# One ring of ten buffers for the u and v rows of the experts, in the order in which GpSimd asks for them

## The chip, the cores and the metric

The kernel runs on one core of one Trainium2 chip. A core has five engines that run their own instruction streams and meet at semaphores: TensorE (PE; its weight loads are listed apart as PEld), VectorE (DVE), ScalarE (ACT), GpSimd (POOL) and SyncE (SP). Sixteen DMA engines move data between HBM and the on-chip memory. The metric is the device time of one execution in microseconds (us); lower is better.

## The reference, cut to what matters

Two layers of a trunk over 256 context and 256 latent tokens of width 1024. Each layer has a block of token mixers and then a layer of experts; in the second layer only the latent tokens go through the experts. The experts are the part that the change touches:

```python
def peer(h, wq, subkeys, u_tab, v_tab):
    ...
    best, pos = lax.top_k(cand, PEER_TOPK)              # 16 experts for each token and each of 8 heads
    idx = jnp.take_along_axis(cidx, pos, axis=-1)       # numbers among 128 * 128 = 16384 experts
    g = jax.nn.softmax(best, axis=-1)
    ...
        act = jax.nn.gelu(jnp.einsum('thkd,td->thk', u_tab[ib], hb))
        return jnp.einsum('thk,thkd->td', (gb * act).astype(v_tab.dtype), v_tab[ib])
```

For every token, head and chosen expert one row of 1024 float32 of the table u is fetched and dotted with the token's activation, and one row of the table v is fetched and added with the weight `g * gelu(dot)`. The tables stay in HBM, 64 MB each for one layer; only the chosen rows are read.

## The kernel before, in words

`build` runs, one after the other: `begin`, `opening` (mixers of layer 0), `experts_beside` (experts of layer 0 for 512 tokens, with the rest of the layer's mixers and the first part of layer 1 woven in), `closing` (the rest of the mixers of layer 1), `experts` (experts of layer 1 for the 256 latent tokens) and `store`. Each of these is a block that ends in a barrier of all engines. In a block each engine has its instructions in a fixed order, written out tick by tick by the parts' methods.

The class `Peer` is the expert layer. 128 tokens lie on the 128 partitions. One tick has two halves: the even half handles the u row number n, the odd half the v row number n - LV, with LV = 20. A row here means one gather: 128 table rows, one to a partition, 128 x 1024 float32, 0.524 MB. In `experts_beside` there are 512 u rows and 512 v rows, in `experts` 256 of each. A window of 16 rows belongs to one head.

- GpSimd issues the gathers, in one stream: `ask_u` (line 1862) and `ask_v` (line 1875). For the first 20 ticks it asks for u rows alone (u0 to u19), then for one u and one v in turn (u20, v0, u21, v1, ...), and for the last 20 for v rows alone.
- VectorE dots each u row with the tokens' activation (`dot`, line 2109, counted by `u_dotted`), and between dots it goes through the choice of the experts of later windows (`choose`, which ends in line 2217 and counts `chosen_done`; the first u row of a window waits for that).
- TensorE adds v rows in pairs (`add_v`, line 2002, counted by `v_summed`, one count for two rows). For the first pair of each window it needs the window's weights, which are transposed by line 1981 and copied by ScalarE (line 2075).
- After the last pair of 128 tokens ScalarE copies the sums (line 2064), TensorE transposes them (lines 1964, 1967) and VectorE adds them to the residual (line 2118). After the last pair of a block this is followed by the barrier and the next block.

Before the change u rows have five buffers and v rows have five others (`RU, RV`). The u row n is asked for once the u row n - 5 has been dotted; the v row v once the pair that holds the row v - 5 has been summed. The projection beside the experts loads its weights on SP's queue (`arena<-in_w_in`, line 565) and multiplies in line 595.

Of the kernel before, what the change touches and what calls it, by code (L numbers as in the profile page):

```python
# [19 lines left out]
P = 128  # L20
D = 1024
# [1706 lines left out]
class Peer(Part):  # L1728
# [3 lines left out]

    RU, RV, LV = 5, 5, 20

    def __init__(self, nc, sems, m, mod, d, l, passes, h, x, banks, after, kept=1):
        self.nc, self.m, self.mod, self.d, self.l, self.passes, self.h, self.x = nc, m, mod, d, l, passes, h, x
        self.after, self.kept = after, kept
        self.QB, self.TB = banks  # L1740
        self.W = 16 * len(passes)
        self.n = 16 * self.W
        self.ticks = 2 * (HEAD + self.n + 34)
        self.kind = [1 if lo < CTX else 0 for lo in passes]
        self.u_rows = d["peer_u"].rearrange("l e n -> (l e) n")
        self.v_rows = d["peer_v"].rearrange("l e n -> (l e) n")
        (self.sk_turned, self.sk_out, self.q_mult, self.q_out, self.s_mult, self.s_out, self.s_used,
         self.diffed, self.g_exp, self.shared, self.chosen_done, self.u_dotted, self.gelu_done,
         self.key_masked, self.rows_known, self.coef_masked, self.spread, self.weights_out,
         self.v_summed, self.h_turned, self.h_out, self.o_copied, self.o_turned, self.o_added, *rest) = sems(  # L1750
             "sk_turned", "sk_out", "q_mult", "q_out", "s_mult", "s_out", "s_used", "diffed", "g_exp",
             "shared", "chosen_done", "u_dotted", "gelu_done", "key_masked", "rows_known",
             "coef_masked", "spread", "weights_out", "v_summed", "h_turned", "h_out",
             "o_copied", "o_turned", "o_added", *[f"wq_in{r}" for r in range(2 * kept)],
             *[f"sk_in{r}" for r in range(2)], *[f"u_in{r}" for r in range(self.RU)], *[f"v_in{r}" for r in range(self.RV)])
        K = 2 * kept
        self.wq_in, self.sk_in, rest = rest[:K], rest[K:K + 2], rest[K + 2:]
        self.u_in, self.v_in = rest[:self.RU], rest[self.RU:]
        self.own = sems.own
        self.turned_keys = self.turned_queries = self.turned_rows = self.turned_out = 0  # L1760
        self.spread_keys = self.spread_coefs = 0
        self.normed = []
        self.choosing = None
# [82 lines left out]
    def gpsimd(self, pool, i):  # L1846
# [4 lines left out]
        else:  # L1851
            self.ask_v(pool, i // 2 - HEAD)

    def ask_u(self, pool, n):
        nc, x = self.nc, self.x
        if 0 <= n < self.n:
            w, q = divmod(n, 16)
            if q == 0:
                pool.wait_ge(self.chosen_done, w + 1)
            if n >= self.RU:  # L1860
                pool.wait_ge(self.u_dotted, n - self.RU + 1)
            nc.gpsimd.indirect_dma_start(x.us[:, n % self.RU, :], None, self.u_rows, bass.IndirectOffsetOnAxis(  # L1862
                x.chosen[:, w, q:q + 1], 0)).then_inc(self.u_in[n % self.RU], 16)

    def ask_v(self, pool, n):
        nc, x = self.nc, self.x
        v = n - self.LV
        if 0 <= v < self.n:
            w = v // 16
            c, r = self.place(v)  # L1870
            if v % 16 == 0:
                pool.wait_ge(self.rows_known, w + 1)
            if v >= self.RV:
                pool.wait_ge(self.v_summed, (v - self.RV) // 2 + 1)
            nc.gpsimd.indirect_dma_start(x.vs[:, v % self.RV, :], None, self.v_rows, bass.IndirectOffsetOnAxis(  # L1875
                x.rows[:, w % 4, 4 * c + r:4 * c + r + 1], 0)).then_inc(self.v_in[v % self.RV], 16)

    def free_turns(self, pe):

# [105 lines left out]
    def add_v(self, pe, n):  # L1985
# [7 lines left out]
        if v % 16 == 1:  # L1993
            pe.wait_ge(self.weights_out, g + 1)
        for a in (v - 1, v):
            pe.wait_ge(self.v_in[a % self.RV], 16 * (a // self.RV + 1))
        flat = x.wts[:, g % 2, :, :].rearrange("p r n -> p (r n)")
        for half in range(2):
            for a in (v - 1, v):
                c, r = self.place(a)  # L2000
                to = 32 * ((c + 2 * half) % 4)
                ins = nc.tensor.matmul(m.ps[to:to + 32, half, :], flat[:, r * P + 32 * c:r * P + 32 * c + 32],  # L2002
                                       x.vs[:, a % self.RV, half * BANK:(half + 1) * BANK], start=a % 128 < 4,
                                       stop=a % 128 >= 124)
        ins.then_inc(self.v_summed, 1)

# [92 lines left out]
    def dot(self, dve, n):  # L2099
        nc, m, x = self.nc, self.m, self.x  # L2100
        if 0 <= n < self.n:
# [2 lines left out]
            g = n // 16  # L2104
            if n % 16 == 0 and g >= 4:
                dve.wait_ge(self.gelu_done, g - 3)
            dve.wait_ge(self.u_in[n % self.RU], 16 * (n // self.RU + 1))
            u, at = x.us[:, n % self.RU, :], 16 * (g % 4) + n % 16
            nc.vector.tensor_tensor_reduce(u, u, x.ht, 1.0, 0.0, ALU.mult, ALU.add, x.dots[:, at:at + 1]  # L2109
                                           ).then_inc(self.u_dotted, 1)  # L2110
        for half, at in ((0, 156), (1, 158)):
# [111 lines left out]

def peer_memory(sb, passes, kept=1):
    x = Mem()
    x.us, x.vs = sb("u_rows", [P, Peer.RU, D]), sb("v_rows", [P, Peer.RV, D])
    x.ht, x.ob = sb("h_rows", [P, D]), sb("out_rows", [P, D])
    x.wq, x.sk, x.skT = sb("wq", [P, kept, 2, KD // 2, T]), sb("subkeys", [P, 2, 2, P]), sb("subkeysT", [P, 2, P])
    x.q0, x.q1 = sb("q0", [P, 2, P]), sb("q1", [P, PH, 2, P])
# [430 lines left out]
```

## Time and profile before

| | us |
|---|---|
| median of 3 runs | 3344.3 (3339.93 to 3347.95) |
| profiled execution | 3360.33, of which 3358.2 lie between its first and its last instruction |
| GpSimd's first u row, `experts_beside` | at 610.75 |
| end of the last v pair there | at 2338.95 |
| GpSimd's first u row, `experts` | at 2624.50 |
| end of the last v pair there | at 3339.38 |

Busy shares of the span: TensorE 69%, VectorE 55%, GpSimd 52%, ScalarE 18%. The 16 DMA engines moved 1028.53 MB at 306 GB/s over the span, 847.35 MB of it on the queue that GpSimd fills. The shares are averages over stages that have different limits, so the stages are read one by one: by the busy time of each engine and the DMA share in chosen stretches of time, by who waited for whom, and by the instructions of an engine in order of time.

### The profile page before, as it was taken

Reading aid. Unit: us, or ns where it says so; the run is one execution under the profiler, and the core shown is the slowest. Engines: PE = TensorE matmul, PEld = TensorE weight load, DVE = VectorE, ACT = ScalarE, POOL = GpSimd, SP = SyncE. Lnnn points to the kernel's source line nnn. Section 1 sums busy time; section 2 is a strip of 40 time slices with the busy share of each in tenths; the row PEclk is TensorE's granted clock in tenths of the full one; section 3 lists DMA queues with packets and bytes.
Section 4 is the critical chain, followed back from the end, with each engine's and each line's share of the span. In section 5 each row is a group of like instructions: output and inputs, shape, how many; then the busy total and the mean of one; then the engine's idle time right before and its main releaser. Section 6 shows DMA issues by size and latency. Waiting matters only on the chain. (4 is left out here: it accounts for less than half of the span.)

```text
span 3358.2 us, 31993 instructions
## 1 busy us (share of the span) xinstructions
PE 2308.6 (69%) x10877; PEld 1384.0 (41%) x10877; DVE 1848.4 (55%) x4792; ACT 617.1 (18%) x1252; POOL 1733.9 (52%) x1580
## 2 busy tenths in 40 slices
PE   5999999878856887565776577554798555444434
PEld 3676677634524654223553255321567322101001
DVE  1324334677775566775546754672434766666651
ACT  2113432124111121111102121110241111110000
POOL 0001000467775566776667666774000577777774
PEclk7999989978668998677887688765788766555555
DMA  7576222899999999999999899997303999999997
GB/s 282 178 267 237 86 63 97 303 365 373 334 374 352 354 383 361 378 370 362 352 343 369 307 396 388 393 379 267 112 1 108 309 395 403 406 389 393 389 380 255
DMA packets 395064, 1028.53 MB, mean 306 GB/s; under 512 B 31890, under 2 KB 176282, under 8 KB 393754
## 3 DMA queue, kind: packets, MB, share of 16 engines
q0 software_dynamic: 232064, 847.35, 66.4%
q1 hardware_dynamic: 162794, 179.15, 16.0%
q8 instruction: 89, 1.46, 0.2%
q14 instruction: 69, 0.57, 0.0%
q10 hardware_dynamic: 48, 0.01, 0.0%
HBM read 1019.05 MB, written 7.34 MB: 306 GB/s over the span
## 5 line engine op out<-in xcount | busy, mean ns | idle before, releaser
L1862 POOL DMA_INDIRECT u_rows<-in_peer_u,chosen x768 | 860.9, 1121 | 866.1 <-DVE chosen L2217 585.3
L2109 DVE CUSTOM_DVE_ANT_0 u_rows<-u_rows,h_rows 128x1024 f32<-128x1024 f32 x768 | 935.8, 1222 | 559.3 <-DMA u_rows<-in_peer_u,chosen 539.6
L1875 POOL DMA_INDIRECT v_rows<-in_peer_v,row_of x768 | 844.0, 1099 | 445.7 <-PE ps L2002 248.9
L2002 PE MATMUL ps<-v_rows,weights 128*32 128x512 f32 x3072 | 588.6, 848 | 697.2 <-DMA v_rows<-in_peer_v,row_of 694.6
L2002 PEld LDWEIGHTS ps<-v_rows,weights 128*32 128x32 f32 x3072 | 76.7, 124 | 978.7 <-issue 959.8
L1556 PE MATMUL ps<-front,arena 128*128 128x256 f32 x1536 | 389.6, 411 | 75.5 <-DMA arena<-in_w_in 74.6
L1556 PEld LDWEIGHTS ps<-front,arena 128*128 128x128 f32 x1536 | 311.9, 207 | 160.4 <-DMA arena<-in_w_in 62.0
L595 PE MATMUL ps<-front,arena 128*128 128x256 f32 (+1 forms) x816 | 202.4, 407 | 45.3 <-DMA arena<-in_w_in 41.4
L1930 PE MATMUL ps<-h,wq 128*128 128x256 f32 x768 | 199.2, 413 | 5.4 <-ACT h L439 3.7
L595 PEld LDWEIGHTS ps<-front,arena 128*128 128x128 f32 (+1 forms) x816 | 160.2, 200 | 91.4 <-issue 35.0
L1930 PEld LDWEIGHTS ps<-h,wq 128*128 128x128 f32 x768 | 155.0, 209 | 55.4 <-issue 31.3
L361 POOL DMA_DIRECT2D arena<-in_ada_w x40 | 28.9, 722 | 287.8 <-PE ps L384 247.0
L1571 ACT COPY arena<-ps 128x256 f32<-128x256 f32 x96 | 35.9, 374 | 327.4 <-PE ps L1556 327.3
L2075 ACT COPY weights<-ps 128x128 f32<-128x128 f32 x48 | 12.8, 267 | 342.7 <-DVE row_of L2152 270.2
L2053 ACT ACTIVATE gelu<-dots 128x16 f32<-128x16 f32 x48 | 10.4, 216 | 344.0 <-DVE dots L2109 343.9
L2118 DVE SCALAR_TENSOR_TENSOR resid<-ps,mod,resid 128x128 f32<-128x128 f32 x48 | 13.5, 344 | 108.4 <-PE ps L1964 86.3
L2035 ACT COPY scores<-ps 128x256 f32<-128x256 f32 x48 | 17.9, 372 | 292.8 <-PE ps L1944 292.8
L629 DVE COPY front<-ps 128x256 f32<-128x256 f32 (+2 forms) x28 | 11.8, 422 | 108.6 <-PE ps L595 98.9
L831 DVE RECIPROCAL arena<-arena 96x512 f32<-96x512 f32 (+2 forms) x21 | 63.9, 3041 | 10.6 <-ACT arena L741 10.1
L943 DVE TENSOR_REDUCE arena<-ps 128x1 f32<-128x512 f32 (+1 forms) x48 | 28.8, 600 | 73.6 <-PE ps L893 73.0
L2020 ACT COPY subkeysT<-ps 128x256 f32<-128x256 f32 x48 | 17.8, 371 | 271.8 <-PE ps L1909 271.8
L1642 PE MATMUL ps<-front,arena 128*128 128x256 f32 x256 | 63.7, 400 | 4.4 <-DVE arena L1658 1.5
(356 smaller groups left out, 3213.4 us busy)
## 6 DMA issues: line engine op xcount, KB each, us to landing
arena<-in_w_in SPq DMA_DIRECT2D x79, 1024.0 KB, 13.6
arena<-in_ada_w POOLq DMA_DIRECT2D x40, 1024.0 KB, 6.6
wq<-in_peer_wq SPq DMA_DIRECT2D x48, 512.0 KB, 9.2
arena<-in_w_out SPq DMA_DIRECT2D x12, 1024.0 KB, 7.3
u_rows<-in_peer_u,chosen POOLq DMA_INDIRECT x768, 6.8
v_rows<-in_peer_v,row_of POOLq DMA_INDIRECT x768, 6.6
ada_w<-in_ada_w SPq DMA_DIRECT2D x4, 2048.0 KB, 23.2
arena<-in_w_branch SPq DMA_DIRECT2D x16, 512.0 KB, 3.6
```

What stands on the lines that cost most here:

```text
L361: pool.dma_start(self.raw[:, j % self.RING, :, :], weights.rearrange("(k p) n -> p k n", p=P)[:, k0:k0 + 2, lo:lo + MROUND]).then_inc(self ...
L595: ins = nc.tensor.matmul(m.ps[0:n, bank, 0:T], w, h[:, k, :], start=(k == 0), stop=(k == KD - 1))
L831: self.own.link(nc.vector.reciprocal(self.tile(x.rs2, j), self.tile(x.rs2, j)))
L943: self.own.link(nc.vector.reduce_max(x.st[:, 2, u:u + 1], m.ps[:, self.S, 0:n], axis=AX.X))
L1556: ins = nc.tensor.matmul(m.ps[:, self.banks[i % 2], 0:T], self.ring[:, (c + self.flip) % 2, k, (i % 2) * P:(i % 2 + 1) * P], self.f.h[:, k ...
L1571: nc.scalar.copy(self.sig[:, j % self.room, :], self.m.ps[:, self.banks[j % 2], 0:T]).then_inc(self.out, 1)
L1642: ins = nc.tensor.matmul(m.ps[:, self.banks[n % 2], 0:T], self.wb[:, n // 4 % 2, a, (k % 4) * P:(k % 4 + 1) * P], self.f.yT[:, i, a, :], s ...
L1862: nc.gpsimd.indirect_dma_start(x.us[:, n % self.RU, :], None, self.u_rows, bass.IndirectOffsetOnAxis(x.chosen[:, w, q:q + 1], 0)).then_inc ...
L1875: nc.gpsimd.indirect_dma_start(x.vs[:, v % self.RV, :], None, self.v_rows, bass.IndirectOffsetOnAxis(x.rows[:, w % 4, 4 * c + r:4 * c + r ...
L1930: ins = nc.tensor.matmul(m.ps[:, self.QB + c, 0:T], x.wq[:, b, part, k, c * P:(c + 1) * P], self.h[:, 4 * part + k, :], start=(part == 0 a ...
L2002: ins = nc.tensor.matmul(m.ps[to:to + 32, half, :], flat[:, r * P + 32 * c:r * P + 32 * c + 32], x.vs[:, a % self.RV, half * BANK:(half + ...
L2109: nc.vector.tensor_tensor_reduce(u, u, x.ht, 1.0, 0.0, ALU.mult, ALU.add, x.dots[:, at:at + 1]).then_inc(self.u_dotted, 1)
```

## The change

The two sets of five buffers become one of ten. The list `asked` holds all rows in the order in which GpSimd asks for them: u alone, then u and v in turn, then v alone. The row at place j of the list uses the buffer j mod 10, and it is asked for once the row at place j - 10 has been used: dotted, if that was a u row, or summed with its pair, if it was a v row. In the middle of the list the place j - 10 is the row of the same kind five before, which is what the row waited for already. In the first 20 places the ring holds u rows alone, so u10 waits for u0 instead of u5; u20 (place 20) waits for u10, v0 (place 21) for u11, and so on up to v4 (place 29) for u19. In the last 20 places v rows alone are asked for, and they wait in turn for the last u rows and for v rows up to ten before.

```diff
-    RU, RV, LV = 5, 5, 20
+    R, LV = 10, 20
...
-        self.u_in, self.v_in = rest[:self.RU], rest[self.RU:]
+        self.row_in = rest
+        self.asked = []
+        for n in range(self.n + self.LV):
+            self.asked += [("u", n)] if n < self.n else []
+            self.asked += [("v", n - self.LV)] if n >= self.LV else []
+        self.place_of = {row: j for j, row in enumerate(self.asked)}
...
+    def take(self, pool, j):
+
+        if j >= self.R:
+            kind, a = self.asked[j - self.R]
+            if kind == "u":
+                pool.wait_ge(self.u_dotted, a + 1)
+            else:
+                pool.wait_ge(self.v_summed, a // 2 + 1)
+
+    def landed(self, j):
+
+        return self.row_in[j % self.R], 16 * (j // self.R + 1)
...
-            if n >= self.RU:
-                pool.wait_ge(self.u_dotted, n - self.RU + 1)
-            nc.gpsimd.indirect_dma_start(x.us[:, n % self.RU, :], None, self.u_rows, bass.IndirectOffsetOnAxis(
-                x.chosen[:, w, q:q + 1], 0)).then_inc(self.u_in[n % self.RU], 16)
+            j = self.place_of["u", n]
+            self.take(pool, j)
+            nc.gpsimd.indirect_dma_start(x.ring[:, j % self.R, :], None, self.u_rows, bass.IndirectOffsetOnAxis(
+                x.chosen[:, w, q:q + 1], 0)).then_inc(self.row_in[j % self.R], 16)
...
-            if v >= self.RV:
-                pool.wait_ge(self.v_summed, (v - self.RV) // 2 + 1)
-            nc.gpsimd.indirect_dma_start(x.vs[:, v % self.RV, :], None, self.v_rows, bass.IndirectOffsetOnAxis(
-                x.rows[:, w % 4, 4 * c + r:4 * c + r + 1], 0)).then_inc(self.v_in[v % self.RV], 16)
+            j = self.place_of["v", v]
+            self.take(pool, j)
+            nc.gpsimd.indirect_dma_start(x.ring[:, j % self.R, :], None, self.v_rows, bass.IndirectOffsetOnAxis(
+                x.rows[:, w % 4, 4 * c + r:4 * c + r + 1], 0)).then_inc(self.row_in[j % self.R], 16)
...
-            pe.wait_ge(self.v_in[a % self.RV], 16 * (a // self.RV + 1))
+            pe.wait_ge(*self.landed(self.place_of["v", a]))
...
-            dve.wait_ge(self.u_in[n % self.RU], 16 * (n // self.RU + 1))
-            u, at = x.us[:, n % self.RU, :], 16 * (g % 4) + n % 16
+            j = self.place_of["u", n]
+            dve.wait_ge(*self.landed(j))
+            u, at = x.ring[:, j % self.R, :], 16 * (g % 4) + n % 16
...
-    x.us, x.vs = sb("u_rows", [P, Peer.RU, D]), sb("v_rows", [P, Peer.RV, D])
+    x.ring = sb("expert_rows", [P, Peer.R, D])
```

No engine has more or fewer instructions, and none changes its order; the semaphores are as many as before. What changes is the semaphore and the count for which GpSimd's gathers wait at the two ends of the list, and the place of a row in memory.

GpSimd at the start of an expert block. The names of the semaphores are those that the same numbers had earlier in the program: m_placed_1 is `chosen_done`, m_in0_1 is `u_dotted`, m_in3_1 is `rows_known`, stored_9 is `v_summed`. A row ending in x11 stands for eleven instructions. Before:

```order
L1862 DMA u_rows<-in_peer_u,chosen 128x1024 [waits m_placed_1]
L1862 DMA u_rows<-in_peer_u,chosen 128x1024 x4
L1862 DMA u_rows<-in_peer_u,chosen 128x1024 [waits m_in0_1] x11
L1862 DMA u_rows<-in_peer_u,chosen 128x1024 [waits m_in0_1,m_placed_1]
L1862 DMA u_rows<-in_peer_u,chosen 128x1024 [waits m_in0_1] x4
L1875 DMA v_rows<-in_peer_v,row_of 128x1024 [waits m_in3_1]
L1862 DMA u_rows<-in_peer_u,chosen 128x1024 [waits m_in0_1]
L1875 DMA v_rows<-in_peer_v,row_of 128x1024
```

and now, at the same place:

```order
L1880 DMA expert_rows<-in_peer_u,chosen 128x1024 [waits m_placed_1]
L1880 DMA expert_rows<-in_peer_u,chosen 128x1024 x9
L1880 DMA expert_rows<-in_peer_u,chosen 128x1024 [waits m_in0_1] x6
L1880 DMA expert_rows<-in_peer_u,chosen 128x1024 [waits m_in0_1,m_placed_1]
L1880 DMA expert_rows<-in_peer_u,chosen 128x1024 [waits m_in0_1] x4
L1893 DMA expert_rows<-in_peer_v,row_of 128x1024 [waits m_in0_1,m_in3_1]
L1880 DMA expert_rows<-in_peer_u,chosen 128x1024 [waits m_in0_1]
L1893 DMA expert_rows<-in_peer_v,row_of 128x1024 [waits m_in0_1]
```

Ten u rows instead of five are asked for before the first dot is waited for, and the first v rows now wait for dots.

GpSimd at the end of an expert block, from the last u row on (u511 in `experts_beside`). Before:

```order
L1862 DMA u_rows<-in_peer_u,chosen 128x1024 [waits m_in0_1]
L1875 DMA v_rows<-in_peer_v,row_of 128x1024 [waits stored_9] x5
L1875 DMA v_rows<-in_peer_v,row_of 128x1024 [waits stored_9,m_in3_1]
L1875 DMA v_rows<-in_peer_v,row_of 128x1024 [waits stored_9] x15
L312 UNCONDITIONAL_BRANCH
```

and now:

```order
L1880 DMA expert_rows<-in_peer_u,chosen 128x1024 [waits m_in0_1]
L1893 DMA expert_rows<-in_peer_v,row_of 128x1024 [waits stored_9]
L1893 DMA expert_rows<-in_peer_v,row_of 128x1024 [waits m_in0_1]
L1893 DMA expert_rows<-in_peer_v,row_of 128x1024 [waits stored_9]
L1893 DMA expert_rows<-in_peer_v,row_of 128x1024 [waits m_in0_1]
L1893 DMA expert_rows<-in_peer_v,row_of 128x1024 [waits stored_9]
L1893 DMA expert_rows<-in_peer_v,row_of 128x1024 [waits m_in0_1,m_in3_1]
L1893 DMA expert_rows<-in_peer_v,row_of 128x1024 [waits stored_9]
L1893 DMA expert_rows<-in_peer_v,row_of 128x1024 [waits m_in0_1]
L1893 DMA expert_rows<-in_peer_v,row_of 128x1024 [waits stored_9]
L1893 DMA expert_rows<-in_peer_v,row_of 128x1024 [waits m_in0_1]
L1893 DMA expert_rows<-in_peer_v,row_of 128x1024 [waits stored_9] x11
```

Five of the last twenty v rows now wait for a dot instead of a sum, and the others for a sum that lies up to ten rows back.

## Rows read from the trace of the kernel before

**Rows 1.** Busy us of engines in three stretches; granted clock, DMA share, GB/s.
```profile
1100.00:1350.00 250.00, 208.16 (x989) 142.03 (x987) 156.08 (x421) 48.92 (x85) 162.27 (x141) 0.90 0.99 369
2349.00:2624.00 275.00, 237.28 (x1083) 180.07 (x1084) 113.44 (x303) 83.90 (x184) 0.00 (x0) 0.83 0.28 94
2680.00:3290.00 610.00, 281.65 (x1200) 84.76 (x1198) 394.25 (x1041) 58.77 (x107) 471.61 (x455) 0.56 1.01 394
```

**Rows 2.** The same view of the two ends, where only v rows are asked for.
```profile
2300.00:2337.00 37.00, 18.82 (x81) 2.22 (x74) 0.29 (x2) 0.27 (x1) 15.94 (x17) 0.55 0.79 271
3300.00:3337.40 37.40, 19.76 (x81) 2.49 (x81) 1.70 (x4) 0.48 (x2) 16.59 (x18) 0.50 0.83 279
```

**Rows 3.** GpSimd's waits, 2295 to 2350: total us, times, longest.
```profile
POOL v_rows L1875 <- PE ps L2002: 15.4, 9, 3.0
```

**Rows 4.** GpSimd at the first end: start, us, engine, line, instruction [idle before].
```profile
2298.11 0.94 POOL L1875 DMA_INDIRECT v_rows<-in_peer_v,row_of  x1 [0.31 <-issue]
2302.03 0.94 POOL L1875 DMA_INDIRECT v_rows<-in_peer_v,row_of  x1 [2.97 <-PE ps L2002]
2303.27 0.94 POOL L1875 DMA_INDIRECT v_rows<-in_peer_v,row_of  x1 [0.30 <-issue]
...
2331.83 0.94 POOL L1875 DMA_INDIRECT v_rows<-in_peer_v,row_of  x1 [1.87 <-PE ps L2002]
```

**Rows 5.** The other engines at the first end, same columns.
```profile
2337.02 1.93 PE L2002 MATMUL ps<-v_rows,weights 128*32 128x512 f32 x8 [1.69 <-DMA v_rows<-in_peer_v,row_of]
2339.01 1.07 ACT L2064 COPY out_rows<-ps 128x512 f32<-128x512 f32 x2 [33.44 <-PE ps L2002]
...
2349.35 1.02 SPq L565 DMA_DIRECT2D arena<-in_w_in  x2
```

**Rows 6.** The second end: GpSimd, TensorE and ScalarE, same columns.
```profile
3303.86 0.94 POOL L1875 DMA_INDIRECT v_rows<-in_peer_v,row_of  x1 [3.22 <-PE ps L2002]
...
3332.84 0.94 POOL L1875 DMA_INDIRECT v_rows<-in_peer_v,row_of  x1 [2.39 <-PE ps L2002]
3337.45 1.93 PE L2002 MATMUL ps<-v_rows,weights 128*32 128x512 f32 x8 [1.95 <-DMA v_rows<-in_peer_v,row_of]
3339.44 1.07 ACT L2064 COPY out_rows<-ps 128x512 f32<-128x512 f32 x2 [32.63 <-PE ps L2002]
```

**Rows 7.** DMA issues: KB each, median us from issue to landing.
```profile
v_rows<-in_peer_v,row_of POOLq DMA_INDIRECT x768, 6.6
```

**Rows 8.** GpSimd's waits, 2624 to 2662: total us, times, longest.
```profile
POOL u_rows L1862 <- DVE dots L2109: 3.8, 2, 2.3
```

**Rows 9.** GpSimd and VectorE at the second start, columns as in rows 4.
```profile
2641.96 0.94 POOL L1862 DMA_INDIRECT u_rows<-in_peer_u,chosen  x1 [0.30 <-issue]
2642.89 1.22 DVE L2109 CUSTOM_DVE_ANT_0 u_rows<-u_rows,h_rows 128x1024 f32<-128x1024 f32 x1 [1.37 <-DMA u_rows<-in_peer_u,chosen]
...
2644.39 0.94 POOL L1862 DMA_INDIRECT u_rows<-in_peer_u,chosen  x1 [1.49 <-DVE dots L2109]
...
2645.81 0.17 DVE L2217 TENSOR_SCALAR chosen<-key 128x16 uint32<-128x16 f32 x1
...
2647.24 1.22 DVE L2109 CUSTOM_DVE_ANT_0 u_rows<-u_rows,h_rows 128x1024 f32<-128x1024 f32 x1
...
2647.59 1.68 POOL L1862 DMA_INDIRECT u_rows<-in_peer_u,chosen  x1 [2.26 <-DVE dots L2109]
```

**Rows 10.** GpSimd's waits from 2662 to 3295, the two largest besides "issue".
```profile
POOL v_rows L1875 <- PE ps L2002: 4.3, 14, 0.3
POOL u_rows L1862 <- PE ps L2002: 3.0, 10, 0.3
```

**Rows 11.** GpSimd's waits, 610 to 656, at the first start.
```profile
POOL u_rows L1862 <- DVE dots L2109: 19.1, 11, 5.3
```

**Rows 12.** Two stretches at the first start, columns as in rows 1.
```profile
612.00:678.00 66.00, 54.46 (x240) 45.84 (x241) 48.57 (x140) 6.04 (x16) 36.21 (x34) 0.89 1.02 371
678.00:690.00 12.00, 12.00 (x56) 9.35 (x56) 2.61 (x4) 2.87 (x6) 3.76 (x4) 0.92 0.56 190
```

**Rows 13.** TensorE and GpSimd there, columns as in rows 4.
```profile
674.20 6.56 PE L595 MATMUL ps<-front,arena 128*128 128x256 f32 x16 [5.17 <-DMA arena<-in_w_in]
684.01 0.94 POOL L1875 DMA_INDIRECT v_rows<-in_peer_v,row_of  x1 [9.81 <-PE ps L2002]
```

More of the change, by code:

```diff
@@ L1754, in __init__ @@
              "o_copied", "o_turned", "o_added", *[f"wq_in{r}" for r in range(2 * kept)],
-             *[f"sk_in{r}" for r in range(2)], *[f"u_in{r}" for r in range(self.RU)], *[f"v_in{r}" for r in range(self.RV)])
+             *[f"sk_in{r}" for r in range(2)], *[f"row_in{r}" for r in range(self.R)])
         K = 2 * kept
         self.wq_in, self.sk_in, rest = rest[:K], rest[K:K + 2], rest[K + 2:]
-        self.u_in, self.v_in = rest[:self.RU], rest[self.RU:]
+        self.row_in = rest
[4 more added lines that the diff above has]
+        self.place_of = {row: j for j, row in enumerate(self.asked)}
         self.own = sems.own
@@ L2002, in add_v @@
                 ins = nc.tensor.matmul(m.ps[to:to + 32, half, :], flat[:, r * P + 32 * c:r * P + 32 * c + 32],
-                                       x.vs[:, a % self.RV, half * BANK:(half + 1) * BANK], start=a % 128 < 4,
+                                       x.ring[:, self.place_of["v", a] % self.R, half * BANK:(half + 1) * BANK], start=a % 128 < 4,
                                        stop=a % 128 >= 124)
```

## The prediction, made before the changed kernel was run

> **What bounds the kernel now.** I read the busy time by stretch first, because the shares of the whole span mix stages. In the middle of both expert blocks the 16 DMA engines are full: DMA share 0.99 at 369 GB/s in the first, 1.01 at 394 GB/s in the second, while TensorE, VectorE and GpSimd all have idle time [rows 1]. There only fewer bytes or a better use of the DMA engines could help, and the change moves the same bytes. `closing`, between them, has a DMA share of 0.28 and no GpSimd at all [rows 1], so the change doesn't reach it except by shifting it.
>
> The same view of the two ends, where only v rows are left, shows something else: share 0.79 at 271 GB/s and 0.83 at 279 GB/s [rows 2]. What GpSimd waits for there is TensorE's sum: 15.4 us in 9 waits at the first end [rows 3], seen one by one in its instructions [rows 4]. TensorE in turn waits for v rows to land [rows 5]. That is a circle of ask, landing, sum, ask, which five buffers don't fill. Both ends lie on the path. At the first, the last pair is summed at 2337.02, ScalarE copies the sums at 2339.01, and the next block's first load goes out at 2349.35 [rows 5]. At the second, ScalarE copies right after the last pair [rows 6] and the kernel ends at 3358.2.
>
> **The change, part by part.** *Middle of the lists: nothing.* With u and v in turn, the row ten places back is the row of the same kind five back, so each gather waits for the same count of the same semaphore as before.
>
> *First end, 11.2 us.* v495 is the first row that is held long: it is asked for at 2302.03 after 2.97 us of idle time [rows 4]. An ask that waits for nothing has 0.30 us ahead of it, so in a ring of ten it goes out 2.67 us sooner, at 2299.36. Sixteen rows follow, and unhindered asks start 1.24 us apart (2302.03, 2303.27) [rows 4]: 16 x 1.24 = 19.8, the last ask at 2319.2 instead of 2331.83. With the median of 6.6 us to landing [rows 7] the last row is there at 2325.8. The last sum began at 2337.02 [rows 5], so 11.2 us are gained. The bytes say the same: 37 us at 271 GB/s are 10.03 MB [rows 2]; at the 394 GB/s of the second block [rows 1] they take 25.5 us, to 2325.5. Does the ring of ten hold anything up? v511 waits for the pair of v501, asked for at 2299.36 + 6 x 1.24 = 2306.8, landed at 2313.4 and summed (1.93 us [rows 5]) at 2315.3, 3.9 us before it is needed. TensorE takes 1.93 us for a pair and the DMA engines 2 x 0.524 MB / 394 GB/s = 2.7 us, so TensorE stays behind the data.
>
> *Second end, 10.1 us.* By the same steps: 3303.86 less 3.22 - 0.30 [rows 6] is 3300.94; plus 19.8 and 6.6 makes 3327.4, against a last sum that began at 3337.45 [rows 6]. By bytes: 37.4 us at 279 GB/s are 10.43 MB [rows 2], 26.5 us at 394, which would give 10.9. I take the smaller figure.
>
> Bounds of the two ends. The upper one is by bytes, 11.5 + 10.9 = 22.4. For the lower one, suppose that more rows in flight fill the idle time of the DMA engines but leave their speed while busy: 271 / 0.79 = 343 and 279 / 0.83 = 336 GB/s [rows 2]. Then 10.03 MB take 29.2 us (7.8 gained) and 10.43 MB take 31.0 (6.4 gained), 14.2 in sum. I take 21.3, since the rate of 394 GB/s was held for 610 us by gathers of the same size on the same queue [rows 1].
>
> The row shows 394 GB/s. The Trainium skill, page "DMA: Bandwidth & Descriptors", section "Bandwidth", puts what HBM gives one core at about 358 GB/s. By that figure the ends would take 28.0 and 29.1 us and gain 9.0 + 8.3 = 17.3 instead of 21.3. The trace of the second block does not agree with it, so I leave it out of the sum.
>
> *Second start, 2.4 us.* With ten buffers for u rows alone, two waits for dots go, 3.8 us in all [rows 8], less 2 x 0.30: 3.2 us. Part of it comes back, for an ask that starts while a dot runs takes longer: 1.68 us at 2647.59, inside the dot that began at 2647.24, against 0.94 at 2644.39, outside [rows 9]. Without its wait, u12 starts at 2641.96 + 1.24 = 2643.20, inside the dot of 2642.89 [rows 9], and pays 0.74. That leaves 2.4; with three asks caught it is 1.0, with none 3.2. Next late would be u16, which waits for the choice of the second window: done at 2645.98 [rows 9], while u13 starts at about 2645.2 and u16 three asks later, so it isn't. The gain stays to the end of the block, because from here to 3295 GpSimd never waits more than 0.3 us for a buffer [rows 10] and the DMA engines are full: rows that come earlier leave fewer bytes.
>
> The row shows an ask being held by a dot. The Trainium skill, page "SBUF — State Buffer", section "SBUF: two separate sides", calls the port that VectorE and GpSimd share an exclusive lock, which blocks the loser until the other's instruction ends. By that rule alone u12 would be held from 2643.20 to the dot's end at 2644.11, 0.91 us, and the term would be 2.3.
>
> *First start, 0 us.* GpSimd waits 19.1 us in 11 waits for dots here [rows 11], and they mostly go. But the DMA engines are full all the same, share 1.02 from 612 to 678 [rows 12], with the projection's weights. Rows asked for sooner only push these back. And a stop for all follows: TensorE waits 5.17 us for weights, up to 674.20, and GpSimd waits 9.81 us for TensorE, up to 684.01 [rows 13]. At that point the ring lets GpSimd be no further than before. Bounds: a gain of 3.9 us if the 66 us ran at 394 instead of 371 GB/s; a loss of 6.6 us if all rows that landed after the weights (GpSimd's last ask ended at 674.2, so up to 680.8 by [rows 7]) came before them. I take zero, because a full DMA share says that the order of the bytes changes and not their sum.
>
> *Everything else* is the same instructions in the same order. The new waits of v0 to v4 for dots cost nothing: v4 waits for u19, and u24, asked for just ahead of it, waited for u19 before.
>
> Sum: 11.2 + 10.1 + 2.4 + 0 = 23.7 us off the profiled execution's 3360.3, which makes 3336.6. That execution lies 16 us above the median of the runs; both ends and the start are short stretches that don't scale with it, so I take the same 23.7 off the median: 3344.3 - 23.7 = **3320.6 us**.
>
> **The rivals.** *The ends stay slow.* More rows in flight don't speed up the busy DMA engines: the lower bound, 14.2 + 2.4 = 16.6, gives 3327.7. For it: the low rate while busy at the ends [rows 2]. Against it: that rate comes with few rows in flight, and 394 with more.
>
> *The ends run at the first block's rate.* At 369 GB/s [rows 1] they take 27.2 and 28.3 us, gain 9.8 + 9.1, and with the start 21.3 in all: 3323.0. Against it: the first block shares the engines with the projection's loads, which the ends don't.
>
> *The change doesn't do what it says at the ends.* If the chain there is set by landing alone, so that ten rows in flight each land that much later, only the second start's 2.4 us remain: 3341.9. For it: TensorE's own waits are all for landings. Against it: the DMA share of 0.79 has room.
>
> *Slower by TensorE's clock in `closing`.* This stage starts some 11 us sooner and its matmuls may fall otherwise on the granted clock, whose mean is now 0.83, between the levels of 1.2 and 2.4 GHz. Its 237.28 us of matmul [rows 1] are 237.28 x 0.83 = 197 us at full clock. At a mean of 0.755 they take 261 us, and the 23.7 are gone: that is the point from which it decides. At 0.72 they take 274, a loss of 36 and a net of 12 or 13: 3356.9. Against it: TensorE goes into the block from the same state, 0.50 in both ends' sums [rows 2], and in the same order.
>
> **How the numbers follow.** Forecast 0.60, slow ends 0.20, first block's rate 0.08, no effect at the ends 0.07, clock 0.05. A measurement of this kernel tells about 0.2% from no change, 6.7 us, so faster means below 3337.6. The first three cases lie there: 0.88; no effect is the same: 0.07; the clock is slower: 0.05. All upper bounds together make 22.4 + 3.2 + 3.9 = 29.5 us, or 3314.8, all lower ones 14.2 + 1.0 - 6.6 = 8.6 us, or 3335.7. The range is 3313 to 3335: it takes in the second case, and the 4 us by which the runs of before scatter at the lower end.
>
> **What would show it.** Right: at both ends GpSimd asks for v rows about 1.24 us apart with no wait for TensorE over 1 us, the DMA share is near 1 at over 370 GB/s up to the last landing, and the last sum of the first end begins about 28 us after the ask that stands at 2298.11 [rows 4] instead of 38.9; at the second start no wait for a dot. Wrong: a DMA share near 1 at 340 GB/s at the ends (slow ends), new waits of GpSimd there, weights of the projection that land after 680 and a longer stop of GpSimd behind them, or a mean clock in `closing` under 0.8.

## The result, and the profile after

The changed kernel takes 3329.99 us (median; 3313.53 to 3341.38) against 3344.3 for the kernel before (3327.97 to 3372.35), timed in turn on one chip. The ratio is 0.9943 with a 95% interval of 0.9924 to 0.9963, so 19 us of 3344 (12 to 25) are gone; the two medians alone lie 14.3 us apart. The forecast was 23.7 us off, 3320.6 us, in a range of 3313 to 3335: the sign and the range hold, the median lies 9 us above the point. The page of after begins with its span; busy time per engine follows, and each engine counts as many instructions as before.

```profile
span 3320.9 us, 31995 instructions
PE 2289.4 (69%) x10877; PEld 1370.5 (41%) x10877; DVE 1850.2 (56%) x4792; ACT 616.8 (19%) x1252; POOL 1741.0 (52%) x1580
```

The profiled execution took 3323.04 us, 37.3 less than the one of before. That is twice what the runs show, and the second profiles of both, 3338.54 and 3329.55 us, differ by 9.0; so the spans must not be subtracted and the difference explained as a whole. The table cuts the traces where each stage ends: *opening* up to the first ask for a u row, each *list* from its first u ask to its last, each *end* from the last u ask to the end of the last v sum, `closing` from there to the next block's first u ask, and the rest. The starts of the two blocks lie in the lists. Both kernels were profiled a second time, and those columns are the measure of what a stage does from one execution to the next.

| us | before | before again | after | after again |
|---|---|---|---|---|
| opening | 610.8 | 605.1 | 603.6 | 603.4 |
| first list | 1681.6 | 1664.8 | 1677.6 | 1678.2 |
| first end | 46.63 | 47.59 | 36.41 | 36.88 |
| `closing` | 285.6 | 288.4 | 281.8 | 287.9 |
| second list | 669.4 | 665.9 | 666.1 | 667.0 |
| second end | 45.47 | 45.80 | 36.54 | 35.68 |
| rest | 18.8 | 18.8 | 18.9 | 18.4 |

Only the ends separate the two kernels: 10.5 us at the first and 9.5 at the second, as means of two profiles each, 20.0 in sum. All else lies within what one kernel scatters by itself (the first list of before alone differs by 17 us). The other 18 us of the profiled pair (opening 7.2, first list 4.0, `closing` 3.8, second list 3.3) are of that kind.

**The ends.** GpSimd at the first end, in the columns of [rows 4]: start, us, engine, line, instruction [idle before]. The first line is the last u row, the last one v511.

```profile
2281.13 0.94 POOL L1880 DMA_INDIRECT expert_rows<-in_peer_u,chosen  x1 [0.30 <-issue]
...
2283.64 0.94 POOL L1893 DMA_INDIRECT expert_rows<-in_peer_v,row_of  x1 [0.30 <-issue]
2284.88 0.94 POOL L1893 DMA_INDIRECT expert_rows<-in_peer_v,row_of  x1 [0.31 <-issue]
2286.12 0.94 POOL L1893 DMA_INDIRECT expert_rows<-in_peer_v,row_of  x1 [0.30 <-issue]
...
2307.26 0.94 POOL L1893 DMA_INDIRECT expert_rows<-in_peer_v,row_of  x1 [0.30 <-issue]
```

The asks start 1.24 us apart from the first to the last. In GpSimd's waits from 2283 to 2330 nothing is left of the 15.4 us for TensorE of [rows 3]:

```profile
POOL expert_rows L1893 <- issue: 6.1, 20, 0.3
POOL expert_rows L1893 <- PE ps L2020: 0.3, 1, 0.3
```

The last two sums of the first end, ScalarE's copy behind them and the next block's first load, against [rows 5]:

```profile
2313.09 1.06 PE L2020 MATMUL ps<-expert_rows,weights 128*32 128x512 f32 x8 [0.70 <-DMA expert_rows<-in_peer_v,row_of]
2315.60 1.94 PE L2020 MATMUL ps<-expert_rows,weights 128*32 128x512 f32 x8 [1.44 <-DMA expert_rows<-in_peer_v,row_of]
2317.59 1.07 ACT L2082 COPY out_rows<-ps 128x512 f32<-128x512 f32 x2 [23.48 <-PE ps L2020]
2327.93 1.01 SPq L565 DMA_DIRECT2D arena<-in_w_in  x2
```

TensorE still waits for landings, but the circle is open: the last two pairs are summed 2.5 us apart, about what the DMA engines need for a pair. By stretch, the first end, `closing`, and the second list (columns as in [rows 1]):

```profile
2286.00:2313.00 27.00, 16.66 (x73) 2.20 (x73) 1.94 (x6) 0.48 (x2) 16.89 (x18) 0.58 1.02 407
2328.00:2599.00 271.00, 233.40 (x1084) 176.95 (x1085) 113.56 (x305) 83.79 (x184) 0.00 (x0) 0.85 0.29 95
2680.00:3260.00 580.00, 264.78 (x1131) 76.20 (x1131) 376.50 (x990) 56.23 (x102) 448.84 (x431) 0.56 1.01 393
```

The first end now runs at DMA share 1.02 and 407 GB/s, where [rows 2] has 0.79 and 271. Over 27 us of the second end, and of both ends of the second profile, it is 1.01 at 393 to 395. `closing` got a mean granted clock of 0.85 (0.83 before), and the list stays at 393 GB/s (394).

**The second start.** The waits for dots of [rows 8] are gone, and u12 goes out at 2618.11, inside the dot that began at 2617.55, so it takes longer, as it was costed (GpSimd and VectorE):

```profile
2616.87 0.94 POOL L1880 DMA_INDIRECT expert_rows<-in_peer_u,chosen  x1 [0.30 <-issue]
2617.55 1.22 DVE L2128 CUSTOM_DVE_ANT_0 expert_rows<-expert_rows,h_rows 128x1024 f32<-128x1024 f32 x1 [1.12 <-DMA expert_rows<-in_peer_u,chosen]
2618.11 1.47 POOL L1880 DMA_INDIRECT expert_rows<-in_peer_u,chosen  x1 [0.31 <-issue]
```

Counted from the block's first ask, u32 is asked for after 66.5 and 66.9 us in the two profiles of after, where the two of before have 71.3 and 70.2. u255, the last u row of this block, comes after 666.1 and 667.0 against 669.4 and 665.9. The gain was there and was lost on the way.

**The first start.** GpSimd's waits from 603 to 690, against [rows 11, 13], and the two stretches that answer to [rows 12]:

```profile
POOL expert_rows L1880 <- DVE dots L2128: 17.9, 4, 9.3
...
POOL expert_rows L1893 <- DVE dots L2128: 6.5, 3, 4.4
POOL expert_rows L1893 <- PE ps L2020: 5.4, 3, 2.3
```

```profile
605.00:671.00 66.00, 53.99 (x228) 45.38 (x227) 40.17 (x120) 6.72 (x18) 34.88 (x30) 0.90 0.95 343
671.00:683.00 12.00, 12.00 (x64) 8.58 (x62) 7.91 (x20) 2.14 (x4) 7.36 (x8) 1.00 0.82 274
```

There are fewer waits for dots than the 11 of before, but longer ones, 24.4 us in all instead of 19.1; the wait of 9.81 us for TensorE is down to 2.3. The first 66 us move less than before (343 GB/s, 371 before) and the next 12 more (274, 190). The two long waits, and the projection's matmul between them, which waits for weights:

```profile
644.18 1.68 POOL L1880 DMA_INDIRECT expert_rows<-in_peer_u,chosen  x1 [7.42 <-DVE dots L2128]
655.50 12.90 PE L595 MATMUL ps<-front,arena 128*128 128x256 f32 x48 [5.36 <-DMA arena<-in_w_in]
666.82 0.94 POOL L1880 DMA_INDIRECT expert_rows<-in_peer_u,chosen  x1 [9.29 <-DVE dots L2128]
```

GpSimd is ahead at first (u20 after 31.0 and 30.6 us, 43.5 and 44.4 before), behind by u32 (91.6 and 87.7; 88.4 and 86.5), and level by u144 (440.9 and 437.0; 440.1 and 437.5).

### The profile page after: what moved, and what is told of

It is laid out like the page before. It is cut to its first block and busy times, and to the rows that moved or that the text cites. A ratio compares the mean times of both kernels' runs of the same rounds, so it can differ in the third digit from the quotient of the medians.

```text
span 3320.9 us, 31995 instructions
## 1 busy us (share of the span) xinstructions
PE 2289.4 (69%) x10877; PEld 1370.5 (41%) x10877; DVE 1850.2 (56%) x4792; ACT 616.8 (19%) x1252; POOL 1741.0 (52%) x1580
## 5 line engine op out<-in xcount | busy, mean ns | idle before, releaser
L1880 POOL DMA_INDIRECT expert_rows<-in_peer_u,chosen x768 | 857.8, 1117 | 853.0 <-DVE chosen L2236 576.2
L2128 DVE CUSTOM_DVE_ANT_0 expert_rows<-expert_rows,h_rows 128x1024 f32<-128x1024 f32 x768 | 936.2, 1222 | 548.0 <-DMA expert_rows<-in_peer_u,chosen 528.5
L1893 POOL DMA_INDIRECT expert_rows<-in_peer_v,row_of x768 | 854.3, 1112 | 409.5 <-PE ps L2020 206.1
L2020 PE MATMUL ps<-expert_rows,weights 128*32 128x512 f32 x3072 | 585.6, 844 | 683.9 <-DMA expert_rows<-in_peer_v,row_of 681.3
L2020 PEld LDWEIGHTS ps<-expert_rows,weights 128*32 128x32 f32 x3072 | 77.0, 125 | 961.9 <-issue 957.2
L831 DVE RECIPROCAL arena<-arena 96x512 f32<-96x512 f32 (+2 forms) x21 | 63.9, 3041 | 10.5 <-ACT arena L741 10.1
L2128 DVE DVE_READ_ACCUMULATOR2_ANT dots<- 128x1 f32 x768 | 62.9, 82 | 0.0
```

The lines of the kernel that those rows point to most:

```text
L831: self.own.link(nc.vector.reciprocal(self.tile(x.rs2, j), self.tile(x.rs2, j)))
L1880: nc.gpsimd.indirect_dma_start(x.ring[:, j % self.R, :], None, self.u_rows, bass.IndirectOffsetOnAxis(x.chosen[:, w, q:q + 1], 0)).then_in ...
L1893: nc.gpsimd.indirect_dma_start(x.ring[:, j % self.R, :], None, self.v_rows, bass.IndirectOffsetOnAxis(x.rows[:, w % 4, 4 * c + r:4 * c + r ...
```

## The experiments

The theory: the time comes from the two ends, where five buffers left the DMA engines idle; the starts give little. The rivals: the gain comes from the starts and their rows in hand; the ends are paced by how long one row takes to land, however many are asked for; or more buffers than ten would give more. Later came a question of the second list: why its start's gain doesn't last.

**The ends alone.** The ring stays; u rows wait at the start for the dot that they waited for with five buffers. In `take`:

```diff
                 pool.wait_ge(self.v_summed, a // 2 + 1)
+        kind, a = self.asked[j]
+        if kind == "u" and 5 <= a < 25:
+            pool.wait_ge(self.u_dotted, a - 4)
```

> The ring of ten as changed, but u5 to u24 wait besides for the dot of the row five before, as they did: only the end of each block is changed. My theory (the two ends and the second start gain independently of each other): from the last u row's ask to the end of the last v sum 36.4 us in the first block and 36.5 in the second, give or take 1 (46.6 and 45.5 in the kernel before); GpSimd waits for dots again at both starts (about 3.8 us at the second); from the first to the last u ask in the second block 669 us as in the kernel before. Whole time 19 us less than before. Rival (what helps at the end is that GpSimd comes there with rows in hand from the start): the ends keep 42 us or more.

It takes 3325.8 us against 3349.72 for the kernel before on the same chip, a ratio of 0.9929 (0.9904 to 0.9954): the whole gain. Its ends take 35.28 and 36.86 us. In GpSimd's waits the wait for dots at the second start is back:

```profile
POOL expert_rows L1883 <- DVE dots L2131: 9.4, 7, 3.0
```

One number was not expected: its second list took 686.9 us, 17 to 21 more than those of before and after (669 was expected). The groups of its second list from 3000 to 3250 show where (line, engine, operation, count | busy us, mean ns | idle before):

```profile
L1896 POOL DMA_INDIRECT expert_rows<-in_peer_v,row_of x88 | 104.7, 1190 | 26.8 <-issue 19.8 <-PE ps L2023 7.0
```

An ask takes 1190 ns on the mean, where an ask outside a dot takes 940. What that is worth is tested below.

**The starts alone.** The other half: the start is free, and the last twenty v rows wait for the pair that they waited for with five buffers.

```diff
+        kind, a = self.asked[j]
+        if kind == "v" and a >= self.n - self.LV:
+            pool.wait_ge(self.v_summed, (a - 5) // 2 + 1)
```

> The ring of ten as changed, but the last 20 v rows wait besides for the sum of the row five before, as they did: only the start of each block is changed. My theory: the ends are as before, 46.6 and 45.5 us, give or take 1; the second block's first to last u ask takes 664 to 667 us, the first block's is within 4 us of 1681.6, so the whole time is 2 to 4 us less than before. Rival (the first start gains too, since GpSimd's waits for dots of 19 us go): the first block's first to last u ask takes 1670 or less, and the whole time falls by 10 or more.

3349.19 us, ratio 1.0004 (0.9983 to 1.0026): no gain, where 2 to 4 us were expected. The ends take 48.65 and 48.96 us, some 5 us more in sum than in the kernel before, where the same to 1 us was expected; why they do stays open. GpSimd's waits at the second end, and its last ask and the last sum:

```profile
POOL expert_rows L1896 <- PE ps L2023: 17.5, 9, 3.5
```

```profile
3325.42 0.94 POOL L1896 DMA_INDIRECT expert_rows<-in_peer_v,row_of  x1 [2.09 <-PE ps L2023]
3330.51 1.94 PE L2023 MATMUL ps<-expert_rows,weights 128*32 128x512 f32 x8 [1.98 <-DMA expert_rows<-in_peer_v,row_of]
```

The second list took 668.4 us, above what the theory gave it, and so here too nothing of the start's gain is seen at its end. With the run before this settles where the time came from: the ends give all of it, the starts nothing that the runs can tell from zero. The interval is 7 us wide to either side and the ends of its profile lost 5, so this run excludes a gain of ten from the starts, as the rival has it, but not one of two or three.

**A dose between.** The same edit with six rows in flight at the ends instead of five.

```diff
-            pool.wait_ge(self.v_summed, (a - 5) // 2 + 1)
+            pool.wait_ge(self.v_summed, (a - 6) // 2 + 1)
```

> The ring of ten, but the last 20 v rows wait besides for the sum of the pair that holds the row six before: three pairs in turn instead of five buffers. My theory (the end is a circle of ask, landing, sum, ask): one pair's turn takes 1.24 for the second ask, 5.2 to landing, 1.93 for the sum and about 0.5 for the signals, 8.9 us for three pairs, 1.48 us for a row against 1.86 before, so an end takes about 40.6 us. Rival (the end needs a deep queue of rows for the DMA engines to reach their full rate): the end stays at 45 us or more and the DMA share there under 0.85.

One run, 3341.57 us. The ends take 42.30 and 41.21 us, between the 45 to 49 of five rows and the 35 to 37 of ten, and 1 to 2 us more than the 40.6 expected. The DMA share is 0.92 at 328 GB/s from 3284 to 3317, over the 0.85 of the rival. GpSimd's waits at the second end, then its last three asks and the last sum:

```profile
POOL expert_rows L1896 <- PE ps L2023: 8.4, 6, 2.6
```

```profile
3309.50 0.93 POOL L1896 DMA_INDIRECT expert_rows<-in_peer_v,row_of  x1 [0.30 <-issue]
3311.88 0.94 POOL L1896 DMA_INDIRECT expert_rows<-in_peer_v,row_of  x1 [1.45 <-PE ps L2023]
3313.12 0.93 POOL L1896 DMA_INDIRECT expert_rows<-in_peer_v,row_of  x1 [0.30 <-issue]
3318.67 1.94 PE L2023 MATMUL ps<-expert_rows,weights 128*32 128x512 f32 x8 [1.11 <-DMA expert_rows<-in_peer_v,row_of]
```

One more row in flight halves the waits (17.5 to 8.4 us) and gives about half of the gain. If more rows in flight only landed that much later each, the sixth buffer would have given nothing.

**More than ten.** Twelve buffers in the second block.

```diff
+        self.R = 12 if kept == PH else 10
...
-    x.ring = sb("expert_rows", [P, Peer.R, D])
+    x.ring = sb("expert_rows", [P, 12 if kept == PH else 10, D])
```

> The ring of ten in the first block, of twelve in the second, where there is memory for it. My theory (with ten, the second end runs at the rate of the DMA engines, one row in 1.28 us, and GpSimd's asks, 1.24 us apart, wait for nothing): the end takes 36.5 us, give or take 1, as with ten, and the first to the last u ask 666 give or take 3. Rival (ten buffers still hold the end up): the end takes 35 us or less.

One run, 3330.21 us; the second end takes 35.84 us (36.54 and 35.68 with ten), the second list 667.0. Ten are enough: with ten, GpSimd already asks every 1.24 us at the ends and waits for nothing, so that more buffers have nothing to take away.

**Both kernels again.** Neither is changed; the question is what repeats.

> The kernel before once more, unchanged: how much its stages scatter from execution to execution. I expect the ends at 46.6 and 45.5 us within 1.5, and the stages that the change doesn't touch (up to the first u ask, from the last v sum of the first block to the first u ask of the second) to scatter by some 7 and 5 us, which is what they differ by between the two kernels' first traces. If they repeat within 1 us instead, the change does something there that I have not seen.

> The changed kernel once more, unchanged: ends 36.4 and 36.5 us within 1.5, the stages that the change doesn't touch scattered as in the kernel before.

3338.54 and 3329.55 us. Their columns stand in the table above: the ends repeat within 1 us, and the other stages differ by more between two executions of the same kernel: the first list of before by 17 us, its opening by 5.7, `closing` of after by 6.1.

**Why the second start's gain is lost.** In the second list of after, behind its start, GpSimd waits for no dot and hardly for a sum, and the DMA engines are full by their share; still a stretch late in it moves fewer bytes than one early in it:

```profile
2700.00:2750.00 50.00, 26.43 (x127) 11.51 (x129) 33.38 (x89) 6.96 (x13) 38.11 (x40) 0.68 1.02 406
3006.00:3060.00 54.00, 20.68 (x87) 4.42 (x86) 34.80 (x101) 4.22 (x8) 42.72 (x38) 0.52 0.97 359
```

The asks for v rows in the first and in the second of these (from the groups: count | busy us, mean ns | idle before):

```profile
L1893 POOL DMA_INDIRECT expert_rows<-in_peer_v,row_of x20 | 18.7, 937 | 6.1 <-issue 6.1
...
L1893 POOL DMA_INDIRECT expert_rows<-in_peer_v,row_of x19 | 25.3, 1334 | 5.8 <-issue 4.0 <-PE ps L2020 1.8
```

A dot and an ask from it, where the ask starts 0.13 us into the dot and lasts 1.91 us:

```profile
3020.51 1.23 DVE L2128 CUSTOM_DVE_ANT_0 expert_rows<-expert_rows,h_rows 128x1024 f32<-128x1024 f32 x1 [1.43 <-DMA expert_rows<-in_peer_u,chosen]
3020.64 1.91 POOL L1893 DMA_INDIRECT expert_rows<-in_peer_v,row_of  x1 [0.31 <-issue]
3022.85 0.94 POOL L1880 DMA_INDIRECT expert_rows<-in_peer_u,chosen  x1 [0.30 <-issue]
```

The theory is that asks start inside dots in some stretches and not in others, and that where they do GpSimd, not the DMA engines, sets the pace. The rival is that the DMA engines are slower there by themselves, and the longer asks only go with it. The test leaves all waits and rows as they are and takes away one thing that the dot has in SBUF: the h row, its second operand, is put into two PSUM banks that are free in the second block.

```diff
         h2, rs, x = sb("h2", [P, KD, T]), sb("rs", [P, T]), peer_memory(sb, 1, PH)
+        x.ht = m.ps[:, 4:6, :].rearrange("p a b -> p (a b)")
```

> The changed kernel, with the activation that the dots of the second block read kept in PSUM instead of SBUF: VectorE then reads one operand of a dot from SBUF, not two. My theory (in the second block's slow stretches the pace is set by GpSimd's asks that are held by dots, 1.33 us in the mean instead of 0.94; a freed port lets all of them take 0.94, and the block runs at 408 GB/s throughout, one u and one v in 2.56 us): first to last u ask in the second block 630 to 645 us instead of 666, asks for v rows 0.94 us in the mean everywhere, the whole time some 25 us under the changed kernel's. Rival (the slow stretches are the DMA engines' own, and asks are long because of them): 660 to 672 us and long asks as before.

3293.09 us against 3349.84 for the kernel before, ratio 0.984 (0.9798 to 0.9882). The second list takes 640.9 us instead of 666 to 667. Its groups from 2700 to 3250, and of after for the same stretch:

```profile
L2128 DVE CUSTOM_DVE_ANT_0 expert_rows<-expert_rows,ps 128x1024 f32<-128x1024 f32 x209 | 255.0, 1220 | 176.8 <-DMA expert_rows<-in_peer_u,chosen 173.4 <-ACT ps L2064 3.4
L1893 POOL DMA_INDIRECT expert_rows<-in_peer_v,row_of x219 | 205.0, 936 | 92.2 <-PE ps L2020 54.9 <-issue 37.2
L1880 POOL DMA_INDIRECT expert_rows<-in_peer_u,chosen x205 | 192.1, 937 | 62.5 <-issue 56.4 <-DVE dots L2128 6.1
```

```profile
L2128 DVE CUSTOM_DVE_ANT_0 expert_rows<-expert_rows,h_rows 128x1024 f32<-128x1024 f32 x206 | 252.4, 1225 | 188.0 <-DMA expert_rows<-in_peer_u,chosen 184.5 <-ACT h_rows L2064 3.4
L1893 POOL DMA_INDIRECT expert_rows<-in_peer_v,row_of x206 | 212.5, 1032 | 62.8 <-issue 56.7 <-PE ps L2020 6.1
```

The dot is as long as it was (1220 and 1225 ns), and the asks take 936 and 937 ns on the mean. The DMA engines run at 406 GB/s from 2680 to 3220, and GpSimd now waits for sums (its waits from 2680 to 3230), as the asks are no longer what is late:

```profile
2680.00:3220.00 540.00, 251.26 (x1089) 71.61 (x1081) 361.85 (x962) 54.09 (x98) 388.37 (x416) 0.57 1.02 406
```

```profile
POOL expert_rows L1893 <- PE ps L2020: 54.7, 96, 1.5
```

So the rival falls: the same DMA engines move the same rows at 406 GB/s once no ask is held. Nor do the dots slow the DMA engines by reading SBUF: from 2700 to 2750 of after they had both operands there too, and the rate was 406. The share of 1.01 in [rows 1] said "full" at 394, and there were 3% behind it.

The theory itself is too narrow. GpSimd's own time over the whole second list, from the first u ask to the last (window, us, busy us of GpSimd with its asks; before, before again, after, after again, this run), shows that it was the limit throughout and not in some stretches only:

```profile
2624.50:3293.91 669.41, 517.00 (x490) 0.57 1.00 385
2605.83:3271.69 665.86, 513.71 (x490) 0.57 1.00 387
2599.34:3265.48 666.14, 516.75 (x491) 0.58 1.00 387
2606.40:3273.39 666.99, 517.62 (x490) 0.58 1.00 386
2591.28:3232.14 640.86, 458.95 (x491) 0.58 1.02 401
```

An ask that waits for nothing has 0.30 us ahead of it, so 490 of them leave GpSimd idle for 147 us. The first four lists have 149.4 to 152.4 us that aren't busy: GpSimd waits for 2 to 5 us in 666 and is otherwise asking. Unheld, 490 asks of 0.94 us would be 461 busy us and not 514 to 518; the rest, 53 to 57 us, is asks held by dots. In this run it is gone, and GpSimd waits for 35 us instead, because now the rows don't land and leave their buffers any faster.

The four runs of this version (3285.22 to 3298.62 us) all lie under the fastest of the changed kernel (3313.53), with which it was not timed in turn. Some 25 of the 37 us between the two medians are the second list; the rest was not traced to a stage, and the other stages scatter by as much.

**The same with the old buffers.** The kernel before with h in PSUM shows what the second start is worth where the middle really is full.

```diff
         h2, rs, x = sb("h2", [P, KD, T]), sb("rs", [P, T]), peer_memory(sb, 1, PH)
+        x.ht = m.ps[:, 4:6, :].rearrange("p a b -> p (a b)")
```

> The kernel before, with the same activation in PSUM and nothing else. With a middle that always runs full, what the second start is worth must show at the end of the list. My theory (the start puts GpSimd 3 to 5 us ahead, and only the uneven pace of the middle hides that): first to last u ask in the second block 3 to 5 us more than with the ring of ten and PSUM. Rival (the gain of the start is lost anyway, because the DMA engines catch up): the same to 1 us. The end of the second block stays at 45 us.

One run, 3327.61 us. Its second list takes 643.6 us, against 640.9 with the ring of ten. From the block's first ask, u20 comes after 31.6 us (27.7 with the ring), u32 after 61.4 (60.4), u144 after 354.8 (352.0), u255 after 643.6 (640.9). Some 2.7 us stay to the end, between the 3 to 5 of the theory and the 1 of the rival. They come from one profile each, and without PSUM the second list of one kernel differs by up to 3.5 us between two executions, so the 2.7 are not shown to be the start's. Its second end takes 47.83 us, again that of five rows.

## Why the prediction was right, and where it was off

*What bounds the kernel.* Right for the ends: the circle of ask, landing, sum, ask was the limit, and six rows halve it, ten end it. Wrong for the second list: the DMA share of 1.01 was taken to mean that nothing but bytes counted there, and GpSimd was said to have idle time. In [rows 1] it is busy for 471.61 us with 455 asks; with 0.30 us ahead of each that is 608 of the 610 us. That this wrong reading cost the forecast so little is luck: the change leaves the middle alone.

*First end, 11.2 us.* 10.2 in the profiled pair, 10.5 over two of each. Its steps can be read from v494, whose ask stands at 2298.11 in [rows 4] and at 2286.12 in after. The seventeen asks behind it came 1.24 us apart, as forecast. From it to the last sum 29.5 us pass (2315.60 - 2286.12), where about 28 were forecast. The term that was mis-sized is the landing: from the last ask to the last sum 8.34 us instead of 6.6. At this end the median from issue to landing is now 7.9 us, the least 6.5 and the most 8.2. That costs 1.7 us; 0.8 came back, since from the last u ask to v494's 5.0 us pass and not 5.8. The landing was taken from [rows 7], a median over the whole kernel. A part of the 1.7 can be worked out from the rows: at 407 GB/s a row of 0.524 MB takes 1.29 us and the asks come every 1.24, so each stands a little further back in the queue, and from the ask at 2291.11 to the last ones the landing grows from 7.8 to 8.2 us. The larger part is a step from 6.7 to 7.8 us between the asks at 2288.61 and 2291.11, and its cause stays open.

*Second end, 10.1 us.* 8.9 in the pair, 10.1 in the second profiles, 9.5 over both. From the last ask to the last sum 7.98 and 6.60 us pass. So the 6.6 of the forecast came once in the four ends of after (8.47 at the first of the second profile): the landing with ten rows in flight is not one number.

*Second start, 2.4 us.* The first steps held: no wait for dots, u12 caught by a dot and 0.53 us longer (0.74 forecast; it began 0.56 us into the dot and not 0.31), u32 3 to 5 us sooner. The step that failed is "the gain stays to the end of the block": over two profiles of each the second list is 667.7 us before and 666.6 after, and the starts alone give a ratio of 1.0004. It failed because GpSimd, not the DMA engines, was the limit of this list: the waits of 0.3 us in [rows 10] are those of an engine that buffers never hold up. The waits that the change takes away did go: GpSimd's time that isn't busy fell by 3 us in both pairs of profiles (152.4 and 152.2 to 149.4 and 149.4). But its busy time rose from 517.0 and 513.7 to 516.8 and 517.6 us, 1.8 us on the mean, as the asks fell otherwise into dots. How much a list loses to dots differs from run to run by more than the gain: by 3.3 us between the two profiles of before, and with 530.4 busy us in the 686.9 of the ends alone. With h in PSUM, 2.7 us remain in one pair of profiles, about the term that was forecast, but not clear of the scatter.

The rows show an ask of 1.91 us inside a dot, and a mean of 0.94 where h is in PSUM. The Trainium skill, page "SBUF — State Buffer", section "SBUF: two separate sides", makes the port pair that VectorE and GpSimd share an exclusive lock, which a VectorE instruction takes in a two-port mode or, against a GpSimd operation that reads SBUF, with two SBUF inputs. The runs agree: with two inputs in SBUF the asks for v rows took 1032 ns on the mean, with one 936. The prediction priced one held ask at the start; held asks are worth ten times as much in the middle, 25 us, where no term was given to them because the change doesn't touch them.

*First start, 0.* The term held (level by u144; the starts alone gave nothing), but not all of its steps. The waits for dots didn't go, they grew from 19.1 to 24.4 us (from 19.9 to 20.9 in the second profiles), and the DMA share was not full all the while (0.95 at 343 GB/s). What held is that the weights and the stop behind them set the pace: GpSimd asked 13 us sooner for u20, and waits of 7.42, 4.42 and 9.29 us for dots took that back.

*The rivals.* Slow ends (DMA share near 1 at 340 GB/s) didn't come: 393 to 407 GB/s. Nor did the first block's rate, for the same reason, nor "no effect at the ends", which the dose of six rows excludes too. The clock in `closing` was 0.85, far from the 0.755 from which it would have decided. (The prediction has 0.50 for TensorE in both ends; [rows 2] shows 0.55 and 0.50, and after has 0.58 at the first.) With h in PSUM the row from 2680 to 3220 shows 406 GB/s. The Trainium skill, page "DMA: Bandwidth & Descriptors", section "Bandwidth", gives the 358 GB/s as a core's part when both cores of an HBM domain stream; no run here has a second core at work, and 406 on one core is above it, so the figure was not the one to price this kernel by.

*The sum.* The ends gave 20.0 of 21.3, the second start about 1 of 2.4, the first start nothing: 21 where 23.7 were forecast. The ratio's 19 us agree with that, and its interval holds both figures. The median's 9 us above the point are then some 3 of mis-sized terms, the rest being the scatter of the medians; that part is inferred and not shown.

## What to carry to other kernels

Where a list ends or one of two streams runs dry, look at the DMA share of just that stretch: a low share with a wait for the consumer means too few buffers in flight, and buffers of the stream that has finished are free to take. A DMA share of 1 doesn't prove that the bytes are the limit: add up the busy time of the engine that asks and the least idle time ahead of each ask, and if that fills the stretch, the asks are the limit. Then compare the GB/s of stretches with the same mix and the mean time of one ask in each. And profile a kernel twice before a difference between two profiles is explained: one pair here gave 37 us, the other 9, for a change worth 19.

## What the runs showed of the hardware

The price of asks held by dots was not expected in this size: with both operands of the dot in SBUF, an ask takes 1.03 to 1.05 us on the mean and up to 2.0; with one operand in PSUM, 0.94, at the same length of the dot (1220 ns). The second list is 25 us shorter with it. An ask that starts within a dot ends 0.81 us after it, wherever in the dot it began: the asks at 2618.11 and 3020.64 of after and at 2647.59 of before [rows 9] began 0.56, 0.13 and 0.35 us into their dots, and each ended 0.81 us behind its dot's end. 0.81 is also the median over all 257 asks of after's second block that start within a dot. Worked out from this, an ask that starts s us into a dot of 1.22 us takes 2.03 - s instead of 0.94, for s up to 1.09: u12, forecast to start 0.31 into its dot, would have paid 0.78, and with 0.56 it paid 0.53.

Ten gathers of 0.524 MB in flight bring the 16 DMA engines to 393 to 407 GB/s in the four ends of after. With five, the two ends ran at 271 and 279, and their landing took 5.2 to 5.5 us at the median where ten take 6.2 to 8.1: the single row lands later and the rows together come faster.
